# A depthwise convolution beside a weight stream: six channel groups on VectorE with sums in PSUM, two on ScalarE and GpSimd

## The reference, cut to what matters

```
proj = h @ w_in                      # h: 256 x 2048, w_in: 2048 x 5120
q, k, v, a, g = split(proj)          # 1024 columns each
u = a * sigmoid(g)                   # 256 tokens x 1024 channels
u = causal_depthwise_conv(u, conv_w, conv_b)   # 31 taps for each channel, plus a bias
u = silu(layer_norm(u, ...))
mix = concatenate([moba_attention(q, k, v), u])
y = mix @ w_out
```

## Time and profile before

| | us |
|---|---|
| median of 3 runs (lowest, highest) | 2349.65 (2349.07, 2350.74) |
| profiled execution, its own time | 2353.44 |
| its span | 2351.7 |
| PE busy in the span | 2274.1 (97%) |
| DVE busy | 1564.4 (67%) |
| ACT busy | 1087.8 (46%) |
| POOL busy | 160.8 (7%) |
| chunks 3 to 9 of `w_in_2` on PE | 1286.40 to 1458.35 |

### The profile page before, as it was taken

How to read it: one execution, slowest core, us unless ns; L and a number is a source line. 1 busy time by engine, 2 the same in 40 slices (tenths; PEclk the granted TensorE clock), 3 DMA queues, 4 the chain that set the end, 5 groups by cost and what they waited for, 6 DMA issues and landing times.

```text
span 2351.7 us, 29348 instructions
## 1 busy us (share of the span) xinstructions
PE 2274.1 (97%) x10344; PEld 1873.4 (80%) x10344; DVE 1564.4 (67%) x1971; ACT 1087.8 (46%) x1520; POOL 160.8 (7%) x178
## 2 busy tenths in 40 slices
PE   8999999999999999999989999898999999999997
PEld 6888777888888888888868777776888888888886
DVE  5445367767777777777776998767777544554545
ACT  5565354544434444344345665636443344434443
POOL 4000000000000000000002774000000000000000
PEclk9999999999999999999989999998999999999999
DMA  6656507788888888888856554575888666666653
GB/s 208 185 178 190 156 25 285 226 260 278 275 281 290 274 274 278 285 285 277 266 171 196 165 168 137 188 259 170 276 277 272 193 189 189 192 191 190 195 179 134
DMA packets 274071, 511.79 MB, mean 218 GB/s; under 512 B 20023, under 2 KB 28389, under 8 KB 273692
## 3 DMA queue, kind: packets, MB, share of 16 engines
q1 hardware_dynamic: 273948, 510.20, 68.4%
HBM read 508.04 MB, written 2.10 MB: 217 GB/s over the span
## 4 chain that ended last, share of the span: by engine, by line
PE 85%; DVE 8%; issue 3%; DMA 2%; ACT 1%; SPq 0%; DVEq 0%; ACTq 0%
PE bank L921 27%; PE bank L923 26%; PE bank L922 26%; DVE w_lo L1663 3%; DVE convT L1620 2%; DMA raw<-in_w_out 1%; PE bank L879 1%; PE bank L952 1%; PE bank L1019 1%; PE bank L939 1%; ACT w_hi L1282 1%; DMA raw<-in_w_in 0%; PE bank L981 0%; ACT ysb L1094 0%; PE bank L893 0%
## 5 line engine op out<-in xcount | busy, mean ns | idle before, releaser
L1663 DVE TENSOR_TENSOR w_lo<-raw,w_hi 128x1024 fp32r<-128x1024 f32 x760 | 942.8, 1244 | 582.8 <-ACT w_hi L1282 573.9
L1282 ACT ACTIVATE w_hi<-raw 128x1024 fp32r<-128x1024 f32 x760 | 802.4, 1059 | 995.1 <-PE bank L923 903.3
L921 PE MATMUL bank<-w_hi,act_hi 128*128 128x512 f32 x2080 | 822.8, 396 | 18.9 <-DVE w_lo L1663 14.5
L923 PE MATMUL bank<-w_hi,act_lo 128*128 128x512 f32 x2080 | 812.9, 391 | 0.0
L922 PE MATMUL bank<-w_lo,act_hi 128*128 128x512 f32 x2080 | 812.8, 391 | 0.0
L921 PEld LDWEIGHTS bank<-w_hi,act_hi 128*128 128x128 f32 x2080 | 392.1, 189 | 108.5 <-DVE w_lo L1663 17.2
L923 PEld LDWEIGHTS bank<-w_hi,act_lo 128*128 128x128 f32 x2080 | 392.2, 189 | 83.4
L922 PEld LDWEIGHTS bank<-w_lo,act_hi 128*128 128x128 f32 x2080 | 392.6, 189 | 79.6 <-issue 0.7
L921 PE MATMUL bank<-w_hi,mid_hi 128*128 128x512 f32 x960 | 379.2, 395 | 6.8 <-DVE w_lo L1663 3.7
L923 PE MATMUL bank<-w_hi,mid_lo 128*128 128x512 f32 x960 | 375.1, 391 | 0.0
L922 PE MATMUL bank<-w_lo,mid_hi 128*128 128x512 f32 x960 | 374.9, 390 | 0.0
(11 more groups left out here) (245 smaller groups left out, 934.0 us busy)
## 6 DMA issues: line engine op xcount, KB each, us to landing
ada_raw<-in_ada_w SPq DMA_DIRECT2D x192, 512.0 KB, 5.2
raw<-in_w_gate SPq DMA_DIRECT2D x176, 512.0 KB, 4.4
raw<-in_w_up SPq DMA_DIRECT2D x176, 512.0 KB, 4.5
raw<-in_w_down SPq DMA_DIRECT2D x176, 512.0 KB, 4.4
raw<-in_w_in SPq DMA_DIRECT2D x168, 512.0 KB, 3.7
raw<-in_w_out SPq DMA_DIRECT2D x64, 512.0 KB, 5.6
x_res<-in_x SPq DMA_DIRECT2D x8, 256.0 KB, 7.3
raw<-in_cmp_w_k SPq DMA_DIRECT2D x4, 512.0 KB, 4.5
```

Source lines behind the costliest of these rows:

```text
L921: pe.matmul(A_[t][:, :], h_, w_hi[:, s, kk, :], start=(k == 0), stop=False)
L923: ins = pe.matmul(A_[t][:, :], l_, w_hi[:, s, kk, :], start=False, stop=(k == KPU * nu - 1))
L1282: act.activation(w_hi[:, U % SPLIT_SLOTS].rearrange("p k n -> p (k n)"), raw[:, R % RAW_SLOTS].rearrange("p k n -> p (k n)"), ACT.Copy).th ...
L1663: dve.tensor_tensor(w_lo[:, U % SPLIT_SLOTS].rearrange("p k n -> p (k n)"), raw[:, R % RAW_SLOTS].rearrange("p k n -> p (k n)"), w_hi[:, U ...
```

## The change

`CONV_POOL` shrinks to groups 2 and 3, so that VectorE has groups 0, 1, 4, 5, 6 and 7: 186 steps instead of 124. ScalarE's products and GpSimd's adds go from 120 to 60, all of them of the first half of the channels: 16 in each of chunks 3 and 4, then 6, 6, 6, 6, 4. VectorE's steps are dealt evenly from chunk 3: 27 in each of chunks 3 to 8, 24 in chunk 9 (within a chunk 4, 4, 4, 3, 3, 3, 3, 3 to a unit). The 62 steps of groups 0 and 1 come first and end in chunk 5; then come groups 4 to 7 tap by tap. The running sums of the first four groups of VectorE (0, 1, 4, 5) lie in the PSUM banks 6 and 7, two groups to a bank, and only the last tap writes the sum to `convT` in SBUF. Those of groups 6 and 7 stay in `convT`. Of the steps in PSUM, those of one group are in place as before: a step reads the sum in its bank and writes it there.

```diff
-    CONV_POOL = [1, 2, 3, 7]
+    CONV_POOL = [2, 3]
     CONV_DVE = [g for g in range(CONV_G) if g not in CONV_POOL]
     CONV_A, CONV_B = 3, 5
     early = [(k, g) for k in range(CONV_K) for g in CONV_DVE if g < 4]
@@
     for i, (n0, cons) in enumerate(IN2):
         cv = []
-        if CONV_A <= i < CONV_B:
-            per = -(-len(early) // (CONV_B - CONV_A))
-            cv = early[(i - CONV_A) * per:(i - CONV_A + 1) * per]
-        if i >= CONV_B:
-            per = -(-len(late) // (len(IN2) - CONV_B))
-            cv = late[(i - CONV_B) * per:(i - CONV_B + 1) * per]
+        if i >= CONV_A:
+            per = -(-(len(early) + len(late)) // (len(IN2) - CONV_A))
+            cv = (early + late)[(i - CONV_A) * per:(i - CONV_A + 1) * per]
@@ conv_step
-                src, wk, o = uT[:, g, k:k + T], conv_w_cols[:, g, k:k + 1], convT[:, g, :]
+                src, wk = uT[:, g, k:k + T], conv_w_cols[:, g, k:k + 1]
+                i = CONV_DVE.index(g)
+                part = MISC[i // 2][:, (i % 2) * T:(i % 2 + 1) * T] if i < 4 else convT[:, g, :]
                 if k == 0:
-                    ins = dve.tensor_scalar(o, src, wk, cols[:, 86 + g:87 + g], ALU.mult, ALU.add)
+                    ins = dve.tensor_scalar(part, src, wk, cols[:, 86 + g:87 + g], ALU.mult, ALU.add)
                 else:
-                    ins = dve.scalar_tensor_tensor(o, src, wk, o, ALU.mult, ALU.add)
+                    o = part if k < CONV_K - 1 else convT[:, g, :]
+                    ins = dve.scalar_tensor_tensor(o, src, wk, part, ALU.mult, ALU.add)
                 ins.then_inc(conv_dve, 1)
                 conv_n[0] += 1
```

## The result

The changed kernel takes 2333.58 us (median of 4, 2330.92 to 2336.24) against 2349.64: a ratio of 0.9934 with a 95% interval of 0.9921 to 0.9947, 16.1 us less. A second series of it gave 2333.12, 0.9928 (0.9914 to 0.9942). The prediction was 2335.0.

What follows compares the result with a forecast made beforehand. VectorE was taken to bound chunks 4 to 9, costing 15.6 us; less 1.0 for unseen waits, 14.6 off the median 2349.65 gives 2335.0. The forecast's own range was 2334.0 to 2338.1, the 8-in-10 range 2333 to 2346.

Steps and rivals of the forecast that it cites:

- The bound, and the 15.6 us: Chunks 4 to 9: VectorE bounds them, TensorE waits for `w_lo` alone; 15.6 us above TensorE's own pace can be had.
- The 1.0 us charged for what could not be seen: Chunks: 1.0 us taken off 15.6 for a few short waits in the units with four taps, leaving 14.6.
- The first sentence on the slices: Slices 21 to 24: VectorE shows 8 and 9 tenths while PE, at full granted clock, drops from 9 to 8.
- Each add holds VectorE once, 0.48: Chunks with GpSimd adding: each add delays one VectorE instruction, 0.48 us for a tap, 0.55 for a `w_lo`.
- A sum in PSUM takes a tap out of it: Taps of groups 0 and 1, chunks 3 and 4: only one operand in SBUF, so taken as untouched by GpSimd.
- What GpSimd costs `w_lo`: Chunks 3 and 4: possible 0 to 4.4 us a chunk, taken 1.1, the add being released when `w_lo` already runs.
- The lead: Entering chunk 3: VectorE's first `w_lo` ends 4.9 us before PE takes it up, eaten before PE waits.
- A tap in PSUM: VectorE taps reading and writing one PSUM bank: no surcharge taken; upper end 0.276 us more each.
- Rival B: Taps reading and writing one PSUM bank are slower, at +0.276 us each: change 11.1 us slower, 2360.8; chance 0.08.
- The 65 ns of the Trainium skill: 124 VectorE taps: PSUM source has a fixed 120 cycles against 58, 65 ns each; loss about 1.4 us.
- Rival A: Operand's place doesn't matter, each add holds VectorE once: loss 11.6 us, gain 4.0, time 2345.6; chance 0.10.
- Behind chunk 9 nothing is tied to a clock, so all of it is passed on: After chunk 9: the whole 14.6 us gained in the chunks reaches the kernel's total time.

## Why the prediction was right

- **The bound, and the 15.6 us.** Right: PE waited for `w_lo` alone and the floor was reached in all seven chunks. The chunk with transposes is 22.65 to 22.69, not 22.56 (chunk 2's 22.66 in the earlier trace rows, with PE never idle, had said so), so 15.1 was to be had in that profile (14.2 and 14.9 in the two others of before). The 1.0 us charged for what could not be seen was not needed; the two misses of 0.5 and 1.0 lie on opposite sides. The first sentence on the slices was misread: in the earlier trace rows PE shows 9 wherever VectorE shows 9, 9, 8, and its 8 is in the slice behind them, which holds the attention. The windows carry the reading alone.
- **Each add holds VectorE once, 0.48.** Right as a price where adds are many (with sums in SBUF VectorE took 57.9 us for chunks 3 and 4, 57.8 counted), too high where they are few (0.42 an add in chunks 5 to 8, where 0.3 was lost and 3.0 counted).
- **A sum in PSUM takes a tap out of it.** Right: 477 ns against 950 for a tap that is held. This one edit is the whole gain; the prediction had summed it together with the moved groups and the even spread, which are worth nothing measurable beside it. Without it they bring some 4 us (2345.78 against 2349.74).
- **What GpSimd costs `w_lo`.** Mis-sized in chunk 3: for half of it the add starts not behind `w_lo` but 0.2 us ahead, and holds it 0.4 us. From start to start the eight `w_lo` steps of chunk 3 are 1.41 long instead of 1.13, 2.2 us in all where 1.1 was taken; in chunk 4 they are 1.22, but there the two `glu` products, with both inputs in SBUF, were held 0.5 each, which was not counted. VectorE took 22.0 and 23.1 us for the two chunks, against 20.9 and 22.7 (from its first `w_lo` at 1279.07 to those at 1301.07 and 1324.15). The lead hid it: the end of a `w_lo` was never less than 2.8 us ahead of the first matmul of its unit (4.2 in the kernel's second profile, so the way in which the two engines meet differs from run to run).
- **A tap in PSUM.** No surcharge: 477 against 474. Rival B (+276) falls. The 65 ns of the Trainium skill ("VectorE: DVE Perf Modes", the section on the TRN2 errata) does not show in this form either: 477 against 474 in the changed kernel, 491 against 484 with GpSimd silent. Only the four first taps, TENSOR_SCALAR, are dearer in PSUM: 531 to 545 against 400 to 415 in SBUF when not held.
- **Rival A** falls by the kernel with PSUM sums alone. Its sum, 2345.6, is what the sums in SBUF give, 2345.8, partly by luck, since its two parts (8.6 and 3.0) came out as 10.5 and 0.3. The rule of the Trainium skill that stands beside it ("SBUF — State Buffer", who interferes with whom) excepts VectorE's two-port modes, which the prediction leaves out. The rows agree with it for the taps and show that one SBUF input is not enough in every form; which mode that form ran in no row shows. A first tap in SBUF, TENSOR_SCALAR with its one tensor input in SBUF, took 824 to 834 ns beside GpSimd's adds (three in the kernel before, three with group 0 alone in PSUM) against 401 alone.
- **"Behind chunk 9 nothing is tied to a clock, so all of it is passed on."** The chunks' gain was passed on; the reason given does not hold, for the attention's length hangs on the granted clock and gave 0.9 to 3.4 us more. Measured 16.1; the means of the three profiles of before and the two of the changed kernel give 171.6 - 156.9 = 14.7 in the chunks and 32.6 - 30.5 = 2.1 in the attention, 16.8, while their whole spans differ by 14.9, since the stretches before and behind vary by some 3 us on their own. The sum had the attention's share at nothing; the 0.5 of the floor and the 1.0 charged for unseen waits partly cancel, so the nearness of 2335.0 to 2333.6 is in part luck.

## What to carry to other kernels

When VectorE and GpSimd work side by side, look at the shortest and the median time of VectorE's two-input instructions: two levels (470 and 956 ns here) mean that GpSimd's instructions hold VectorE, here about once each, and moving one of the two inputs to PSUM frees it at no cost. Count the hold by the other engine's instructions, not by a share of time. Before moving work between engines, try the cheapest part of the change alone: here one edit in one place was all of it, and the work moved beside it only used up VectorE's slack.

## What the runs showed of the hardware that was not expected

- A VectorE SCALAR_TENSOR_TENSOR of 128x256 that reads and writes the same PSUM bank costs about what it does in SBUF: 491 against 484 ns with GpSimd silent.
- TENSOR_SCALAR of 128x256 is held by GpSimd's adds with a single input in SBUF: 824 to 834 ns instead of 400 to 415. In PSUM it took 531 to 545 with GpSimd adding or silent.
- GpSimd holds VectorE for 0.4 to 0.55 us by an add that takes 0.74; an add that starts while `w_lo` runs gets on only when `w_lo` is done (1.73 us for one that began 0.5 us into it).
- Lost time of TensorE in chunks 5 to 9 cost more than itself: the granted clock fell to 1.2 GHz within the attention behind it in seven profiles of seven, and in none of the five that lost 0.3 us or less there. One of these five had such a drop 25 us behind the attention.
